# The first mixer's projections as pairs of seven half-size products, with a weight ring of four slots there

## What is computed

```python
h = rmsnorm(x, norm_mix_pre[i])
z = h @ w_in[i]
xr, gr, q, kc, vc, ksl, vsl, kw, vw, g_nsa, gm_rnn, gm_attn = jnp.split(z, IN_SPLITS, axis=-1)
xr = causal_conv(xr, conv_w[i], conv_b[i])
y_rnn = rg_lru(xr, lru_wa[i], lru_ba[i], lru_wx[i], lru_bx[i], lru_lambda[i]) * jax.nn.gelu(gr)
kc_c = compress(kc.reshape(kv_shape), cmp_pos_k[i], cmp_k_w1[i], cmp_k_w2[i])
vc_c = compress(vc.reshape(kv_shape), cmp_pos_v[i], cmp_v_w1[i], cmp_v_w2[i])
y_attn = nsa(q, kc_c, vc_c, ksl.reshape(kv_shape), vsl.reshape(kv_shape), ...)
y = jax.nn.sigmoid(gm_rnn) * y_rnn + jax.nn.sigmoid(gm_attn) * y_attn
```

## Time and profile before

| | us |
|---|---|
| median of 3 runs | 3061.6 (3060.3 to 3063.1) |
| the profiled execution | 3064.5 |
| its span, first to last instruction | 3062.6 |
| TensorE busy | 2715.5 (89%) |
| VectorE busy | 1141.4 (37%) |
| ScalarE busy | 654.9 (21%) |
| GpSimd busy | 312.2 (10%) |
| mean granted TensorE clock | 0.939 of full |

### The profile page before, as it was taken

The page is one execution under the profiler, slowest core; times in us unless marked ns, Lnnn a source line. Parts: engine busy times, 40 slices in busy tenths (PEclk is TensorE's granted clock), DMA queues, the critical chain, the costliest instruction groups (busy, mean ns, idle before and its releaser), DMA issues. The chain is left out here.

```text
span 3062.6 us, 43424 instructions
## 1 busy us (share of the span) xinstructions
PE 2715.5 (89%) x16618; PEld 1653.0 (54%) x16619; DVE 1141.4 (37%) x2326; ACT 654.9 (21%) x1327; POOL 312.2 (10%) x389
## 2 busy tenths in 40 slices
PE   7999999999999998999977999989788993898755
PEld 3445556578885484557554545445544642454323
DVE  2430157437889932227152111011422624232114
ACT  3440148421100010108131000000221621010002
POOL 0000012004441000000001100000100001122100
PEclk9999989999999999999988999999899996899887
DMA  5223120119545641120027889999632015999994
GB/s 201 83 83 101 53 97 29 59 56 259 198 161 199 259 181 59 55 90 1 28 75 296 346 352 412 397 413 382 256 126 89 1 63 204 370 364 377 404 418 170
DMA packets 137313, 594.52 MB, mean 194 GB/s; under 512 B 20336, under 2 KB 40588, under 8 KB 90608
## 3 DMA queue, kind: packets, MB, share of 16 engines
q1 hardware_dynamic: 86704, 359.25, 31.0%
q10 hardware_dynamic: 41808, 212.75, 17.3%
q0 software_dynamic: 8688, 21.00, 1.9%
HBM read 574.06 MB, written 33.69 MB: 198 GB/s over the span
## 5 line engine op out<-in xcount | busy, mean ns | idle before, releaser
L159 PE MATMUL psum<-normed,weight_ring 128*128 128x512 f32 (+1 forms) x896 | 365.2, 568 | 12.3 <-PEq L174 7.6
L159 PEld LDWEIGHTS psum<-normed,weight_ring 128*128 128x128 f32 x896 | 171.6, 192 | 201.4 <-issue 198.2
L1203 DVE SCALAR_TENSOR_TENSOR psum<-weight_ring,condition_rows 128x1024 f32<-128x1024 f32 x192 | 267.7, 1394 | 16.0 <-issue 0.9
L159 PE MATMUL psum<-modulated,weight_ring 128*128 128x384 f32 (+2 forms) x640 | 228.7, 518 | 0.0
L2469 PE MATMUL psum<-weight_ring,slot_rows_turned 128*32 128x256 f32 x2176 | 143.5, 409 | 73.3 <-DMA weight_ring<-in_w_dram 46.8
L2622 DVE COPY expert_hidden_turned<-psum 128x128 f32<-128x128 f32 (+1 forms) x93 | 32.7, 352 | 466.9 <-PE psum L2480 466.9
L2458 PE MATMUL psum<-weight_ring,slot_rows_turned 128*64 128x256 f32 x1792 | 205.3, 382 | 0.6 <-issue 0.6
L159 PEld LDWEIGHTS psum<-modulated,weight_ring 128*128 128x128 f32 x640 | 121.4, 190 | 105.5 <-issue 51.0
L2458 PEld LDWEIGHTS psum<-weight_ring,slot_rows_turned 128*64 128x64 f32 x1792 | 127.5, 138 | 76.0 <-issue 16.8
L2487 PE MATMUL psum<-weight_ring,expert_hidden_turned 128*32 128x256 f32 (+1 forms) x1536 | 168.0, 445 | 0.0
L2550 ACT ACTIVATE expert_silu<-psum 64x256 f32<-64x256 f32 (+1 forms) x91 | 34.6, 380 | 604.6 <-PE psum L2458 322.6
(11 more groups left out here) (444 smaller groups left out, 3791.7 us busy)
## 6 DMA issues: line engine op xcount, KB each, us to landing
third_stream_weights<-in_w_dram ACTq DMA_DIRECT2D x93, 2048.0 KB, 14.2
weight_ring<-in_w_dram SPq DMA_DIRECT2D x84, 2048.0 KB, 17.1
weight_ring<-in_w_ada_dram SPq DMA_DIRECT2D x24, 2048.0 KB, 8.9
weight_ring<-in_w_ffn_dram SPq DMA_DIRECT2D x11, 2048.0 KB, 12.8
weight_ring<-in_w_rnn_dram SPq DMA_DIRECT2D x8, 1536.0 KB, 11.8
weight_ring<-in_w_att_dram SPq DMA_DIRECT2D x6, 2048.0 KB, 8.0
weight_ring<-in_w_in_dram SPq DMA_DIRECT2D x6, 2048.0 KB, 12.8
weight_ring<-in_w_down_dram SPq DMA_DIRECT2D x8, 1408.0 KB, 6.4
```

The costliest lines, as they stand in the source:

```text
L159: last = nc.tensor.matmul(out, weights[:, k * P:(k + 1) * P], rhs(k), start=(k == 0), stop=(k == tiles - 1))
L1203: last = v.scalar_tensor_tensor(out=product, in0=w[:, t], scalar=1.0, in1=CR[:, n, :], op0=ALU.mult, op1=ALU.mult, accum_out=c.mod[:, i // ...
```

## The change

Two tiles of outputs (weights A, in quarters A11, A12 of the first tile, A21, A22 of the second; tokens B in quarters by feature half and token half) are made by seven products of half the width and half the depth, in place of eight, with sums on other engines:

- `token_sums`: VectorE makes four sums of token quarters once, T1 to T4, kept in the ring's sixth slot.
- `weight_sums`: GpSimd makes four sums of weight quarters per pair (S1, S2, one in place, S4), kept in the ring's fifth slot, for two pairs in turn; it waits for the pair before the last.
- `pair_products`: TensorE's seven products of 8 records each; `first_read`, `whole_read`, `crossed` and `diagonal` are its waits for the other engines' reads.
- `read_first`, `inner_sums`, `outer_sums`: one copy on ScalarE and five additions on VectorE, which put the results together.

The mixer's order is now one plain projection (xr of tile 0), then for each two tiles a gate pair (gr and gm of tile j), a convolution pair (xr of tiles j+1 and j+2; the last one is xr of tile 7 with the first compression input) and a gate pair (j+1), each gate pair followed by its gate matmuls; then a pair of compression inputs ("keys") and one plain projection: 13 pairs. The attention inputs have 6 pairs: two of keys, four of queries. The ring has four slots up to chunk 18 and six from 19 on. The compression's inputs are written, inside the mixer's block, to a buffer that is now allocated before the mixer (`cmp_probs_turned`, used later for the scores; also for two gate tiles of the mixer's output). SyncE's wait before the swapped copy of them is gone. Several semaphores of later stages are re-used ones.

```diff
-    SLOTS = 6
+    SLOTS, EARLY_SLOTS = 6, 4
+    EARLY = 19
...
+    def slot(self, n):
+        if n < self.EARLY:
+            return (n + 1) % self.EARLY_SLOTS
+        return (n - self.EARLY + self.EARLY_SLOTS) % self.SLOTS
+    def before(self, n):
+        if n < self.EARLY:
+            return n - self.EARLY_SLOTS
+        i = n - self.EARLY - (self.SLOTS - self.EARLY_SLOTS)
+        return -1 if i < 0 else self.EARLY - self.EARLY_SLOTS + i if i < self.EARLY_SLOTS else n - self.SLOTS
+    def turn(self, n):
+        return 0 if n < 0 else 1 + self.turn(self.before(n))
...
+            if self.before(n) >= 0:
+                sp.wait_ge(*self.last_use[self.before(n)])
+            sp.dma_start(dst, src).then_inc(self.landed[self.slot(n)], 16)
...
+FIRST, SIXTH, SEVENTH, FIFTH, WHOLE, FOURTH, THIRD = range(1, 8)
...
+def token_sums(c, dve, x):
+    f, v = c.pairs, c.nc.vector
+    B11, B12, B21, B22 = quarters(x)
+    v.tensor_tensor(f.T1, B12, B11, ALU.subtract)
+    v.tensor_tensor(f.T3, B22, B12, ALU.subtract)
+    dve.drain()
+    v.tensor_tensor(f.T2, B22, f.T1, ALU.subtract)
+    dve.drain()
+    v.tensor_tensor(f.T4, f.T2, B21, ALU.subtract).then_inc(f.token_sums.sem, 1)
+def weight_sums(c, pool, p, top, bottom):
+    f, g = c.pairs, c.nc.gpsimd
+    A11, A12, A21, A22 = top[:, 0:KH * P], top[:, KH * P:], bottom[:, 0:KH * P], bottom[:, KH * P:]
+    if p >= 2:
+        f.product.wait(pool, 7 * (p - 1))
+    g.tensor_tensor(f.S1(p), A21, A22, ALU.add).then_inc(f.weight_sums.sem, 1)
+    pool.drain()
+    g.tensor_tensor(f.S2(p), f.S1(p), A11, ALU.subtract).then_inc(f.weight_sums.sem, 1)
+    g.tensor_tensor(A21, A11, A21, ALU.subtract).then_inc(f.weight_sums.sem, 1)
+    pool.drain()
+    g.tensor_tensor(f.S4(p), A12, f.S2(p), ALU.subtract).then_inc(f.weight_sums.sem, 1)
+def pair_products(c, pe, p, top, bottom, x):
+    f = c.pairs
+    B11, B12, B21, B22 = quarters(x)
+    def product(to, weights, rhs, starts=True, stops=True):
+        for k in range(KH):
+            last = c.nc.tensor.matmul(to, weights[:, k * P:(k + 1) * P], rhs[:, k], start=(starts and k == 0),
+                                      stop=(stops and k == KH - 1), skip_group_check=not (starts and stops))
+        last.then_inc(f.product.sem, 1)
+    if p >= 2:
+        f.whole_read.wait(pe, p - 1)
+    product(f.bank1(p), top[:, 0:KH * P], B11, stops=False)
+    f.weight_sums.wait(pe, 4 * p + 2)
+    product(f.bank6, f.S2(p), f.T2)
+    f.weight_sums.wait(pe, 4 * p + 3)
+    product(f.bank7, bottom[:, 0:KH * P], f.T3)
+    if p >= 1:
+        f.crossed.wait(pe, p)
+    product(f.bank5, f.S1(p), f.T1, stops=False)
+    f.first_read.wait(pe, p + 1)
+    product(f.bank1(p), top[:, KH * P:], B21, starts=False)
+    product(f.bank4, bottom[:, KH * P:], f.T4)
+    f.diagonal.wait(pe, p + 1)
+    f.weight_sums.wait(pe, 4 * p + 4)
+    product(f.bank5, f.S4(p), B22, starts=False)
+def read_first(c, act, p, scale=1.0):
+    f = c.pairs
+    f.product.wait(act, 7 * p + FIRST)
+    if p >= 2:
+        f.crossed.wait(act, p - 1)
+    c.nc.scalar.mul(f.U2(p), f.bank1(p), scale).then_inc(f.first_read.sem, 1)
+def inner_sums(c, dve, p, to22, scale=1.0):
+    f, v = c.pairs, c.nc.vector
+    f.first_read.wait(dve, p + 1)
+    f.product.wait(dve, 7 * p + SIXTH)
+    v.scalar_tensor_tensor(out=f.U2(p), in0=f.bank6, scalar=scale, in1=f.U2(p), op0=ALU.mult, op1=ALU.add)
+    dve.drain()
+    f.product.wait(dve, 7 * p + SEVENTH)
+    v.scalar_tensor_tensor(out=f.U3, in0=f.bank7, scalar=scale, in1=f.U2(p), op0=ALU.mult, op1=ALU.add)
+    dve.drain()
+    f.product.wait(dve, 7 * p + FIFTH)
+    v.scalar_tensor_tensor(out=to22, in0=f.bank5, scalar=scale, in1=f.U3, op0=ALU.mult, op1=ALU.add)\
+        .then_inc(f.diagonal.sem, 1)
+def outer_sums(c, dve, p, to21, to12, scale=1.0):
+    f, v = c.pairs, c.nc.vector
+    f.product.wait(dve, 7 * p + FOURTH)
+    v.scalar_tensor_tensor(out=to21, in0=f.bank4, scalar=-scale, in1=f.U3, op0=ALU.mult, op1=ALU.add)
+    f.product.wait(dve, 7 * p + THIRD)
+    v.scalar_tensor_tensor(out=to12, in0=f.bank5, scalar=scale, in1=f.U2(p), op0=ALU.mult, op1=ALU.add)\
+        .then_inc(f.crossed.sem, 1)
 
...
+        order = [step for j in range(0, KT, 2) for step in (("gate", j), ("conv", j + 1), ("gate", j + 1))]
+        order.append(("keys", 1))
...
+        def halves(kind, j):
+            if kind == "gate":
+                return (j, 1), (j, 2)
+            if kind == "keys":
+                return (KT, j), (KT, j + 1)
+            return (j, 0), ((KT, 0) if j == KT - 1 else (j + 1, 0))
...
+                for p, step in enumerate(order):
+                    (n, t), (m, u) = halves(*step)
+                    weight_sums(c, pool, p, wide(n)(ring.take(pool, n=n))[t], wide(m)(ring.take(pool, n=m))[u])
...
+                project(nc, ps[:, 7, :], wide(0)(ring.take(pe, n=0))[0], lambda k: H[:, k, :]).then_inc(c.att_z_ready, 1)
+                f.token_sums.wait(pe, 1)
+                for step in order:
+                    kind, j = step
+                    pair(step)
+                    if kind == "gate":
+                        ring.used(f.product.sem, 7 * (at[step] + 1), n=j)
+                        if j == 0:
                             pe.wait_ge(gates_w, 64)
+                        pe.wait_ge(xc_ready, j + 1)
+                        if j >= 1:
+                            pe.wait_ge(gates_read, j)
+                        nc.tensor.matmul(ps[:, 6, :], WG[:, 0, j, :], XC[:, j % 2, :], start=True, stop=True)
+                        nc.tensor.matmul(ps[:, 7, :], WG[:, 1, j, :], XC[:, j % 2, :], start=True, stop=True)\
                             .then_inc(gates_ready, 1)
+                f.whole_read.wait(pe, len(order) - 1)
+                project(nc, ps[:, 4 + len(order) % 2, :], wide(KT)(ring.take(pe, n=KT))[3], lambda k: H[:, k, :])\
+                    .then_inc(c.att_z_ready, 1)
+                ring.used(c.att_z_ready, 2, n=KT)
...
+                act.wait_ge(c.att_z_ready, 1)
+                nc.scalar.copy(XR[:, 0, CONV - 1:], ps[:, 7, :]).then_inc(z_read, 1)
+                read_first(c, act, 0)
+                for j in range(KT):
+                    p, follows = at["gate", j], after[j]
+                    act.wait_ge(gates_ready, j + 1)
                     if j >= 1:
+                        act.wait_ge(tile_done, j)
+                    nc.scalar.activation(R[:, :], ps[:, 6, :], ACT.Sigmoid, bias=c.vec("lru_ba", j))
+                    nc.scalar.activation(I[:, :], ps[:, 7, :], ACT.Sigmoid, bias=c.vec("lru_bx", j))\
+                        .then_inc(gates_read, 1)
+                    read_first(c, act, p + 1)
+                    act.drain()
+                    if j == 0:
+                        act.wait_ge(lam_v, 2)
+                    nc.scalar.activation(A[:, :], R[:, :], ACT.Exp, scale=lam[:, 4, j:j + 1])
+                    nc.scalar.activation(TH[:, :], R[:, :], ACT.Tanh, scale=lam[:, 5, j:j + 1]).then_inc(a_ready, 1)
+                    act.wait_ge(m_ready, j + 1)
+                    nc.scalar.activation(B[:, :], M[:, :], ACT.Sqrt).then_inc(s_ready, 1)
+                    gr, gm = outputs("gate", j)
+                    nc.scalar.activation(gr[:, half(0)], f.bank1(p), ACT.Gelu_apprx_tanh).then_inc(f.whole_read.sem, 1)
+                    f.crossed.wait(act, p + 1)
+                    nc.scalar.activation(gr[:, half(1)], gr[:, half(1)], ACT.Gelu_apprx_tanh)
+                    nc.scalar.activation(gm, gm, ACT.Sigmoid).then_inc(mix_gates, 1)
+                    if follows[0] != "gate":
+                        copy_whole(follows)
+                    if follows[0] == "conv":
+                        read_first(c, act, p + 2)
+                act.wait_ge(c.att_z_ready, 2)
+                nc.scalar.copy(KCV[:, 3, :], ps[:, 4 + len(order) % 2, :])
...
+                conv(0)
+                inner(("gate", 0))
+                outer(("gate", 0))
+                for j in range(KT):
+                    follows = after[j]
+                    if follows[0] == "gate":
+                        conv(j + 1)
+                    dve.wait_ge(a_ready, j + 1)
+                    v.tensor_tensor(HS[:, :], A[:, :], A[:, :], ALU.mult)
+                    dve.drain()
+                    v.scalar_tensor_tensor(out=M[:, :], in0=HS[:, :], scalar=1.0, in1=TH[:, :],
+                                           op0=ALU.add, op1=ALU.mult).then_inc(m_ready, 1)
+                    v.tensor_tensor(I[:, :], I[:, :], XC[:, j % 2, :], ALU.mult)
+                    inner(follows)
+                    dve.wait_ge(s_ready, j + 1)
+                    dve.drain()
+                    v.tensor_tensor(B[:, :], B[:, :], I[:, :], ALU.mult)
+                    dve.drain()
+                    v.tensor_tensor_scan(HS[:, :], A[:, :], B[:, :], 0.0, ALU.mult, ALU.add)
+                    outer(follows)
+                    gr, gm = outputs("gate", j)
+                    dve.wait_ge(mix_gates, j + 1)
```

(24 more changed lines are left out.)

304 lines of the change are left out of this document (140 added, 164 removed).

## The result

| | before | after |
|---|---|---|
| median of the runs, us | 3060.9 (3060.0 to 3063.1, 4 runs) | 3040.9 (3036.5 to 3041.1, 4 runs) |
| profiled execution, its span | 3064.5, 3062.6 | 3041.0, 3039.2 |
| TensorE, VectorE busy in the span | 2715.5, 1141.4 | 2687.7, 1225.9 |
| ScalarE, GpSimd busy in the span | 654.9, 312.2 | 652.6, 418.8 |

A forecast was written before the change was run, and what follows sets the result against it. TensorE alone bounds the mixer and attention inputs. Gain 32.7 us less costs of 10.5 (2.5, 3.0, 0.5, 0.4, 3.1, 1.0) nets 22.2, taking the median from 3061.6 to about 3039.5 us; range 3031 to 3050.

The forecast's parts named there:

- The products: Mixer and attention inputs: two projections as seven products save 1.65 us a pair, 31.3 us for 19 pairs, plus 1.4 us.
- Token sums: First pair of the mixer: TensorE waits 2.5 us (0 to 2.8) for VectorE's sums, which take turns with GpSimd.
- Steady state: Mixer's groups of three pairs: VectorE's additions, held by GpSimd's sums, come late, 0.75 us a group, 3 us (0 to 9).
- The two other places: Mixer, after the second and the first gate pair: VectorE's additions are done with 0.7 and 0.1 us to spare.
- Small gaps and end of the mixer: Mixer: 0.5 us for small gaps, and 0.4 us because ScalarE reads the last projection inside the stage.
- Start of attention: Second product of the attention inputs: TensorE waits 3.1 us (2.9 to 4.0) for GpSimd's first two sums, behind two clearings.
- Clock: After the wait opening the attention inputs, TensorE at half clock loses 1 us (0 to 2.6).
- Rival D: Whole kernel: a later stage that doesn't start earlier takes the gain back, within 3 us of before; chance 0.05.
- rival A: Whole kernel: no clash between VectorE and GpSimd matters; net gain 28.2 us, about 3033.5 us; chance 0.13.
- Ring, late bias: Four-slot weight ring: chunk reuse is covered; a delayed bias of the compressed scores is hidden behind TensorE's turned scores.
- The moved buffers and re-used semaphores: Buffers moved in SBUF and semaphores used again add nothing on TensorE: 0 us.

The follow-up runs named there:

- e_sum_twice: Kernel after, with one more 128x512 sum by GpSimd into an unread buffer in each of the mixer's pairs: 3041.9 us, ratio 0.9930 to before.
- e_ring_four: Kernel before, with only the weight ring changed to four slots up to chunk 18 and six from there: 3062.6 us, ratio 1.0000 to before.
- e_both_first: Kernel after, with token sums ahead of lambda's small products and GpSimd's first attention sums ahead of its clearings: 3033.2 us, ratio 0.9914 to before.

## Why the prediction was right, and where only its sum was

Forecast 3039.5 (3031 to 3050), measured 3040.9; the profiled execution 3041.0 against 3042.3. The kinds of cost were right, but their sizes were too large by 6 us (10.5 forecast; 1.19 + 0.04 + 2.64 + 0.6 measured), and a cost of like size was missing. That the sum came within 1.4 us of the median is luck: the two errors cancel.

- **The products**: 13 pairs x 1.65 + 1.4 = 22.9 us for the mixer. Measured 21.5 with the token wait of 1.19 in it: the price of 12.08 us a pair holds (a group is 39.70 us, forecast 39.7).
- **Token sums**: 1.19 us instead of 2.5 (0.8 to 1.7 in the other profiles with the same order and sums; the longer the first projection, the shorter the wait). The engines do take turns: a second 128x8 product is held up too (1.23 us), and three of the four sums take 2.13 to 2.28 us instead of 1.21. That is about 1 us lost to each GpSimd sum; I had counted 1.27, and the fourth sum ended at 37.3 instead of 38.5.
- **Steady state**: 0 instead of 3 us, the largest miss. The count gave the `diagonal` product 0.4 us late; its additions were done 0.18 us early. The step that was mis-sized is the price of a turn: that the engines wait out one another's operations, which the prediction took as the sign that something in each group would be late, is so, and nothing was late. The turns are where they were forecast, but an operation lost only 0.86 to 0.92 us to a sum that I had counted at 1.27. e_sum_twice shows how near it was: one more sum makes it late. The 0.75 us a group was a guess over a sum with an error of about 0.5 us to either side. The two other places had 1.6 and 0.5 us to spare (forecast 0.7 and 0.1).
- **Small gaps and end of the mixer**: 0 and 0.04 us instead of 0.5 and 0.4.
- **Start of attention**: 2.64 us instead of 3.1; the order of the events was as forecast. Attention was worth 7.0 to 7.1 us without half clock, forecast 6.8.
- **Clock**: 1.0 us behind that wait. It is 0 in five of the eight profiles and 1.7 us in three, a mean of 0.6. Right in kind, but the large effect lies elsewhere.
- **Rival D, in part.** Without half clock the two stages give 21.5 + 7.1 = 28.6 us, as rival A had it (28.2), and the whole kernel gained 20 to 23.6 on its three chips. Mean half clock in attention over its eight profiles is 4.3 us, 0.9 more than before. The rest takes 2694.7 us as the mean of the three profiles of the unchanged kernel after, and 2689.7 and 2688.6 in the two with the mixer of before: 5.6 us longer, in instructions that are the same. 28.6 - 0.9 - 5.6 = 22.1. Of this the three profiles lose 2.4 to 2.6 us between 1227 and 1392 us of before, where before and e_ring_four lose nothing; for the remainder no single place was found. An estimate from windows of 4 us over the whole rest, (1 - granted clock) x TensorE busy, gives 84.8 and 83.7 us for before and e_ring_four and 87.5, 90.2 and 87.4 for the three: about 4 of the 5.6 us are half clock. But e_sum_twice, with all of the change, has the shortest rest of all (2686.5), so the profiles are too few to say how much of it belongs to the change. I gave 0.05 to "taken back later" in full; a part of it, for the most part by the clock, was not in the sum.
- **Ring, late bias**: nothing, as forecast (e_ring_four; the row at 388.68). The moved buffers and re-used semaphores were put at 0 too; no run changes them alone, so whether they have a share in the 5.6 us stays open.

## What to carry to other kernels

Cost such a change by stage and check it by the distance between two rows of TensorE, less the half clock between them, which repeats within 0.4 us here, and not by the time of the whole kernel, whose intervals are 3 to 5 us to either side. When sums go to GpSimd, list for each wait what VectorE reads: products with two SBUF sources are held by a sum (0.86 us) and not by a clearing, additions with a PSUM source are not held by a sum, and a `tensor_scalar` on SBUF is held by both (1.31 us instead of 0.54 beside a sum, 1.78 instead of 0.17 beside a clearing). Put work that the next product waits for ahead of clearings and small products; here this brought 3.5 us of TensorE's time for moving three lines (e_both_first). TensorE's wait for the token sums stands ahead of the first product of the first pair, which multiplies the plain quarters and takes 1.73 us; behind it, the wait of 1.19 us should vanish too (an estimate, not run).
